# Output projection of a hybrid decoder block in seven quadrant products, on one Trainium2 core

## The chip, the cores and the metric
The kernel runs on one core of a Trainium2 chip. The metric is the device time of one execution in microseconds, the median of several runs. The engines are TensorE (PE, its weight load PEld), VectorE (DVE), ScalarE (ACT), GpSimd (POOL) and SyncE (SP), which here only issues transfers. Transfers issued by SP go over one queue of the core's 16 DMA engines, those issued by GpSimd over another.

## The reference
One decoder block on 512 tokens of width 1024, in float32. What matters here is the end of the mixer and what comes behind it:
```python
merged = jax.nn.sigmoid(gate_r) * y_ret + jax.nn.sigmoid(gate_m) * y_m
return merged @ w_out                      # (512, 1024) @ (1024, 1024)
...
x = x + mixer(...)                         # then RMSNorm, and per token:
group_prob = softmax(xf @ w_group + b_group)          # top 1 of 4 groups
e_logits = xf @ w_expert_router + b_expert_router     # top 2 of 8 experts in it
# per expert: (silu(xb @ w_gate[e]) * (xb @ w_up[e])) @ w_down[e], weighted and added to x
```
Before the mixer's end stand a wide input projection, a retention and an mLSTM, each with a branch projection of 1024 x 1024. There are 32 experts with 1024 x 512, 1024 x 512 and 512 x 1024 weights: 201 MB of float32, read once.

## The kernel before
A float32 product is made of three matmuls on rounded operands: each operand is split into a head (rounded to float32r, on ScalarE) and a tail (the rest, on VectorE), and head x head, head x tail and tail x head are added up in PSUM.

Weights for the projections stream in chunks of 512 x 512 (1 MB) over SP's queue into three places (`raw_mix`). Each half of a chunk (256 x 512, two slices of 128 rows) is a ring entry: `mix_head(q)` on ScalarE writes the head to `wh`, `mix_tail(q)` on VectorE the tail to `wl`, both in a ring of `RING` = 4 entries, running `LEAD` = 3 entries ahead of TensorE. An entry's place in the ring is free when TensorE has used the entry four before it (`entry_used`). A block is 512 output columns: 4 entries (j), 4 tiles of 128 rows (i), with the PSUM banks `pj[0..3]`. Blocks 16 to 21 are the branch projections `B_WR`, `B_WM` and the output projection `B_WO`, two blocks each. The projection blocks before them (`FAST`) already run in another form: a 1024 x 1024 product is cut into quadrants and made of seven products of quadrants (`U_11` to `U_T4`, Winograd's form of Strassen's method), 14 entries in place of 16 per pair of blocks, and four sums of weight quadrants each, some on VectorE (`weight_sum`), one by a transfer issued on GpSimd that adds to its place while it lands (`accum_op`).

When a block of `B_WM` ends, VectorE gates its four tiles into `sgm`, adds them into `mrg` (channels x tokens, 8 slices of 128 channels), ScalarE makes the heads `mrgTh` and VectorE the tails `mrgTl`, tile by tile (`merged_tail`). The two blocks of `B_WO` multiply these with `w_out`; VectorE adds each bank to the stream `x2`, tile by tile, at the end of each block. Then TensorE turns the four tiles of the stream (`turn_stream`, 8 turns each), VectorE and ScalarE copy the turned tiles to `h2T`, `logits(u)` makes the router's logits for half of the tokens, ScalarE copies them, `logit_rows(u)` turns them back. A routing chain on VectorE and TensorE makes the tables of the experts' tokens.

Experts are worked off in 16 pairs. A pair needs 12 chunks of 1 MB: 4 of `w_gate`, 4 of `w_up`, 4 of `w_down`. 22 places of 8 KB per partition (`raw_moe`) and one more (`guest`, for chunk 4) take them; chunk m goes to place m, one lower above 4, and the places lie on memory of tensors that are dead by then: `mrg`, the ring, `mrgTh` and so on. SP issues chunks in a written order (`moe_chunk`), each after a wait for what lay there. SP's instructions are strictly in order, so a wait holds back all chunks behind it. From chunk 22 on a chunk waits until TensorE has used the one 22 before it. The stream is also stored to DRAM (`x_dram`), from where GpSimd gathers each pair's tokens.

## Time and profile before

| | us |
|---|---|
| median of 3 runs (1022.3 to 1024.0) | 1023.38 |
| the profiled execution | 1022.9 |
| its span, first to last instruction | 1021.0 |
| TensorE busy | 996.3 (98%) |
| VectorE, ScalarE, GpSimd busy | 500.1, 323.9, 120.8 |
| DMA | 269.28 MB, mean 264 GB/s |

Times in the rows are from the start of the span. The profiled execution's own time is 1.9 us over its span, so a difference in the span is one in the time. The time falls into the projections with the mixers (to 535 us), the router (to 561) and the experts. The mean granted clock of TensorE is 0.996 of full speed. Matmuls are pipelined, so a busy TensorE may still be waiting for its operands in part; the DMA share is the mean over the 16 engines.

### The profile page before, as it was taken

The numbers are of one execution on the slowest core, as the hardware profiler recorded it, in microseconds if no ns is written. First come the engines' busy times: TensorE is split into PE (matmuls) and PEld (weight loads), VectorE is DVE, ScalarE is ACT, GpSimd is POOL, SyncE is SP. The second block draws the span as 40 slices with busy tenths as digits, with TensorE's granted clock in tenths as the row PEclk, the third lists the DMA queues.
The fourth block names the chain that finished last, engine by engine and source line by source line (L and its number), as shares of the span: only waits on it lengthen the run. The fifth ranks groups of instructions, "written<-read, shape, count | busy, mean of one in ns | idle before, by whom it ended". The sixth has DMA issues, their size and how long they took to land.

```text
span 1021.0 us, 13126 instructions
## 1 busy us (share of the span) xinstructions
PE 996.3 (98%) x4917; PEld 644.4 (63%) x4917; DVE 500.1 (49%) x810; ACT 323.9 (32%) x531; POOL 120.8 (12%) x152
## 2 busy tenths in 40 slices
PE   8999999999999999999998999999999999999896
PEld 7888788889889988888885333333333333333332
DVE  6268646597778677735525123333223233332235
ACT  6344535586556557622213100000000000000012
POOL 0683077000000000000000000000000000000000
PEclk9999999999999999999999999999999999999999
DMA  9223231344334525162988899999999999999993
GB/s 331 83 83 126 92 114 21 83 125 145 66 91 113 185 42 205 43 213 90 422 307 357 348 420 420 420 420 420 420 420 420 421 420 420 420 421 421 421 414 146
DMA packets 63125, 269.28 MB, mean 264 GB/s; under 512 B 9488, under 2 KB 9680, under 8 KB 38360
## 3 DMA queue, kind: packets, MB, share of 16 engines
q1 hardware_dynamic: 57464, 257.32, 63.6%
q0 software_dynamic: 5344, 11.02, 4.9%
q8 instruction: 41, 0.67, 0.3%
q14 instruction: 20, 0.16, 0.0%
q10 hardware_dynamic: 256, 0.10, 0.0%
HBM read 268.41 MB, written 4.20 MB: 267 GB/s over the span
## 4 chain that ended last, share of the span: by engine, by line
PE 72%; SPq 17%; DVE 5%; DMA 3%; ACT 2%; issue 1%; DVEq 0%; ACTq 0%
PE pj L674 23%; PE pj L854 18%; PE pj L956 12%; SPq L575 11%; PE pj L982 6%; SPq L572 6%; PE cb L631 3%; DMA raw_moe<-in_w_up_dram 3%; PE cb L992 2%; PE cb L993 1%; DVE mkT L1758 1%; DVE wl L1494 1%; PE cb L723 1%; PE cb L695 1%; ACT wh L1136 1%
## 5 line engine op out<-in xcount | busy, mean ns | idle before, releaser
L956 PE MATMUL pj<-raw_moe,xT 128*64 128x512 f32 x1016 | 227.6, 595 | 4.2 <-DMA raw_moe<-in_w_up_dram 2.4
L1494 DVE TENSOR_TENSOR wl<-raw_mix,wh 128x1024 fp32r<-128x1024 f32 x116 | 146.2, 1262 | 130.9 <-ACT wh L1136 130.6
L1970 DVE TENSOR_TENSOR x<-x,cb 128x512 f32<-128x512 f32 x120 | 77.0, 683 | 190.2 <-PE cb L993 190.2
L956 PEld LDWEIGHTS pj<-raw_moe,xT 128*64 128x64 f32 x1016 | 72.1, 137 | 140.8 <-issue 140.8
L1136 ACT ACTIVATE wh<-raw_mix 128x1024 fp32r<-128x1024 f32 x116 | 122.4, 1057 | 111.4 <-PE pj L674 68.5
L982 PE MATMUL pj<-raw_moe,hf 128*64 128x512 f32 x512 | 116.7, 598 | 1.6 <-ACT hf L1440 1.6
L982 PEld LDWEIGHTS pj<-raw_moe,hf 128*64 128x64 f32 x512 | 34.6, 136 | 67.2 <-issue 67.0
L1445 ACT ACTIVATE yh<-pj,now 128x512 fp32r<-128x512 f32 x32 | 20.4, 683 | 157.6 <-PE cb L993 143.6
L1440 ACT ACTIVATE hf<-cb 128x512 f32<-128x512 f32 x16 | 9.6, 598 | 146.3 <-PE cb L631 146.3
L992 PE MATMUL cb<-yh,hot 128*128 128x512 f32 x124 | 55.2, 445 | 0.0
L674 PE MATMUL pj<-wh,hTh 128*128 128x512 f32 x128 | 50.8, 397 | 1.7 <-DVE hTl L1525 0.7
L1975 DVE TENSOR_TENSOR xT<-cb,nwc 128x512 f32<-128x512 f32 x32 | 21.9, 687 | 58.0 <-PE cb L631 58.0
L674 PE MATMUL pj<-wl,hTh 128*128 128x512 f32 x128 | 49.9, 390 | 0.0
L674 PE MATMUL pj<-wh,hTl 128*128 128x512 f32 x128 | 49.9, 390 | 0.0
L993 PE MATMUL cb<-yl,hot 128*128 128x512 f32 x124 | 49.2, 397 | 0.0
L1436 ACT ACTIVATE sg<-pj,now 128x512 f32<-128x512 f32 x16 | 11.0, 688 | 100.7 <-PE pj L956 90.0
L992 PEld LDWEIGHTS cb<-yh,hot 128*128 128x128 f32 x124 | 23.6, 190 | 29.0 <-issue 26.2
L854 PE MATMUL pj<-wh,hTh 128*128 128x512 f32 x96 | 39.0, 406 | 0.7 <-DVE mva L1811 0.7
L854 PE MATMUL pj<-wl,hTh 128*128 128x512 f32 x96 | 37.6, 391 | 0.0
L854 PE MATMUL pj<-wh,hTl 128*128 128x512 f32 x96 | 37.4, 390 | 0.0
L854 PE MATMUL pj<-hTh,wh 128*128 128x256 f32 x128 | 36.5, 285 | 0.0
L1986 DVE SCALAR_TENSOR_TENSOR sg<-pj,now,sg 128x512 f32<-128x512 f32 x16 | 12.0, 751 | 49.5 <-PE pj L956 49.5
(397 smaller groups left out, 1858.5 us busy)
## 6 DMA issues: line engine op xcount, KB each, us to landing
raw_moe<-in_w_gate_dram SPq DMA_DIRECT2D x64, 1024.0 KB, 26.7
raw_moe<-in_w_down_dram SPq DMA_DIRECT2D x64, 1024.0 KB, 26.7
raw_moe<-in_w_up_dram SPq DMA_DIRECT2D x63, 1024.0 KB, 26.0
raw_mix<-in_w_in_dram SPq DMA_DIRECT2D x31, 1024.0 KB, 5.3
raw_mix<-in_w_in_dram POOLq DMA_DIRECT2D x10, 512.0 KB, 5.8
raw_mix<-in_w_ret_branch_dram SPq DMA_DIRECT2D x4, 1024.0 KB, 5.8
raw_mix<-in_w_mlstm_branch_dram SPq DMA_DIRECT2D x4, 1024.0 KB, 5.5
raw_mix<-in_w_out_dram SPq DMA_DIRECT2D x4, 1024.0 KB, 5.1
```

The lines of the kernel that those rows point to most:

```text
L572: sp.dma_start(weights_of(m)[:, :, :].rearrange("p (f c) n -> p f (c n)", f=2), w_down[0][e].rearrange("(a p f) n -> p a f n", a=2, f=2)[: ...
L575: sp.dma_start(weights_of(m)[:, :, :], (w_gate, w_up)[kind][0][e].rearrange("(a p k) n -> p a k n", a=2, k=4)[:, half, :, :]).then_inc(lan ...
L631: return nc.tensor.transpose(o, i, kc[0:k, K_IDENT:K_IDENT + k])
L674: m = nc.tensor.matmul(pj[:, i, :], lhsT, rhs, start=k == 0 and n == 0, stop=k == KD - 1 and n == 2)
L854: m = nc.tensor.matmul(o, lhsT, rhs, start=u in (U_11, U_21, U_T1) and k == 0 and c == 0 and n == 0, stop=k == 3 and n == 2, skip_group_ch ...
L956: mm = nc.tensor.matmul(pj[a * CAP:(a + 1) * CAP, up, :], xT[:, 4 * half + k, a * CAP:(a + 1) * CAP], weights_of(m + a)[:, k, :], start=ha ...
L982: mm = nc.tensor.matmul(pj[a * CAP:(a + 1) * CAP, 2 + c, :], hf[:, 2 * half + f, a * CAP:(a + 1) * CAP], weights_of(m + a)[:, 2 * f + c, : ...
L992: nc.tensor.matmul(bank, hot[:, t * P:(t + 1) * P], yh[:, c * 512:(c + 1) * 512], start=begin, stop=False)
L993: return nc.tensor.matmul(bank, hot[:, t * P:(t + 1) * P], yl[:, c * 512:(c + 1) * 512], start=False, stop=True)
L1136: nc.scalar.activation(wh[:, q % RING, :, :], entry_source(q), ACT.Copy).then_inc(wh_ok, 1)
L1494: V.tensor_tensor(wl[:, q % RING, :, :], entry_source(q), wh[:, q % RING, :, :].bitcast(F32), ALU.subtract).then_inc(wl_ok, 1)
L1970: V.tensor_tensor(part, part, cb[:, 2 + g % 2, :], ALU.add).then_inc(c_add, 1)
```

## The change
The output projection is no longer two blocks but seven products of quadrants, 14 ring entries. TensorE takes them in the order `U_11`, `U_21`, `U_T1`, `U_22`, `U_T2`, `U_T3`, `U_T4`, each for two tiles of 128 tokens (s). Activations now are seven parts, split whole (128 x 1024 elements) in place of tile by tile: `out_part_head(n)` on ScalarE, `out_part_tail(n)` on VectorE. Four of them are sums or differences of merged parts: VectorE makes two (`out_part_sum`), and GpSimd two more from them (`combined`, 4 operations each).

Of the weights seven places are loaded: four products' bases go to places of the experts' chunks (`out_slot`: 12, 13, 0, 1) during the branch projections, three to `raw_mix`. Seven sums (`out_sums`) are made by 14 transfers of half a chunk, issued on GpSimd, each after the one before has landed. No sum of weights is on VectorE.

The chunks' order on SP is rewritten to the places' new lives: chunks 13, 14, 0 and 1 come after the entries that use their places, 7 and 8 after the seventh tail, and so on. The results of four quadrants are collected in PSUM and in the stream by VectorE; two banks pass through a copy (`t1c`) on ScalarE. Two tiles of the stream are turned inside `U_T3`, the first logits are made inside `U_T4`.
```diff
 FAST_HALVES = FAST_ENTRIES
-ENTRIES = 4 * (BLOCKS - 2 * len(FAST)) + FAST_ENTRIES
+OUT0 = 4 * (BLOCKS - 2 * len(FAST)) + FAST_ENTRIES
+ENTRIES = OUT0 + 2 * PRODUCTS
...
-                   enumerate([64, 72, 0, 8, 16, 24, 80, 88, 144.0625, 152.0625, 104, 120, TOP, TOP + 8, 32, 40, 48, 56, 96, 112, 194.5625, 186.0625])]
+                   enumerate([64, 72, 0, 8, 16, 24, 80, 88, 144.0625, 152.0625, 96, 112, TOP, TOP + 8, 32, 40, 48, 56, 104, 120, 194.5625, 186.0625])]

...
+        out_slot = {U_11: 12, U_T1: 13, U_T2: 0, U_T4: 1}
+        out_sums = (U_T1, U_T2, U_T2, U_T4, U_T4, U_T4, U_T3)
+
+        def out_place(u):
+
+            return raw_moe[out_slot[u]] if u in out_slot else raw_mix[slot_of(2 * B_WO + (U_T3, U_22, U_21).index(u))]
...
+            def out_load(u, c):
+
+                sp.dma_start(out_place(u)[:, :, :], w_out[0][0:512, 512 * c:512 * (c + 1)].rearrange("(k p) n -> p k n", p=P))\
+                    .then_inc(moe_in[out_slot[u]], 16)
...
+            for n in range(2 * B_WR, 2 * B_WO + 3):
+                if n == 2 * B_WR + 3:
+                    sp.wait_ge(full[1], full_fast(len(FAST) - 1, U_T2, 1))
+                    out_load(U_11, 0)
+                    out_load(U_T1, 1)
+                if n == 2 * B_WR + 4:
+                    sp.wait_ge(tr_ps, KD)
+                    out_load(U_T2, 1)
+                    out_load(U_T4, 1)
                 if n == 2 * B_WM + 2:
...
-            moe_chunk(13, 0, False)
-            moe_chunk(14, 0, False)
             sp.wait_ge(it_ok, 1)
             moe_chunk(21, 0, False)
-            sp.wait_ge(tr_ps, KD)
-            moe_chunk(0, 0, False)
-            moe_chunk(1, 0, False)
-            sp.wait_ge(full[3], full_of(3, B_WO - 1))
-            for m in (2, 3, 5, 6):
-                moe_chunk(m, 0, False)
-            sp.wait_ge(mgl_ok, KD)
+            sp.wait_ge(wl_ok, out_entry(U_11, 1) + 1)
+            moe_chunk(13, 0, False)
+            sp.wait_ge(wl_ok, out_entry(U_T1, 1) + 1)
+            moe_chunk(14, 0, False)
+            sp.wait_ge(mgl_ok, 7)
             moe_chunk(7, 0, False)
             moe_chunk(8, 0, False)
-            sp.wait_ge(wl_ok, ENTRIES)
+            sp.wait_ge(wl_ok, out_entry(U_T2, 1) + 1)
+            moe_chunk(0, 0, False)
+            sp.wait_ge(*out_full(U_T2, 1))
+            for m in (2, 3, 5):
+                moe_chunk(m, 0, False)
+            sp.wait_ge(tr_l, 2 * KD + 2)
+            moe_chunk(6, 0, False)
+            sp.wait_ge(wl_ok, out_entry(U_T3, 1) + 1)
             moe_chunk(9, 0, False)
             moe_chunk(10, 0, False)
-            sp.wait_ge(*entry_used(ENTRIES - 3))
-            for m in (11, 12, 15, 17):
-                moe_chunk(m, 0, False)
             for t in range(TT):
-                sp.wait_ge(free[t], free_of(t, BLOCKS - 1))
+                sp.wait_ge(*tile_ready(t))
                 sp.dma_start(x_dram[t * P:(t + 1) * P, :], x2[:, t, :]).then_inc(st_in, 16)
-            for m in (16, 18, 19, 20):
+                if t == 1:
+                    sp.wait_ge(wl_ok, out_entry(U_T4, 1) + 1)
+                    moe_chunk(1, 0, False)
+                    sp.wait_ge(*out_full(U_T3, 1))
+                    moe_chunk(15, 0, False)
+                    moe_chunk(17, 0, False)
+            for m in (11, 12, 16, 18, 19, 20):
                 moe_chunk(m, 0, False)
             sp.dma_start(irow[:, :], consts[:, K_ROW:K_ALL]).then_inc(br_in, 16)
             sp.wait_ge(lg_ps, 2)
...
                 m.then_inc(lg_ps, 1)

-            pe.wait_ge(tr_l, 2 * KD)
-            for t in range(TT):
-                turn_stream(t)
-            pe.wait_ge(wrt_ok, 1)
-            logits(0)
+            out_parts = ((mrgTh[:, low, lower], mrgTl[:, low, lower]), (mrgTh[:, high, lower], mrgTl[:, high, lower]), (e5h, e5l), (e3h, e3l), (s2h, s2l),
+                         (mrgTh[:, low, upper], mrgTl[:, low, upper]), (mrgTh[:, high, upper], mrgTl[:, high, upper]))
+
+            def out_half(u, s):
+
+                if u == U_11:
+                    pe.wait_ge(*out_free(s, 0))
+                if u == U_21:
+                    pe.wait_ge(*out_free(2 + s, 0))
+                if u == U_22:
+                    pe.wait_ge(tr_h, 2 * KD + s + 1)
+                if u in (U_T2, U_T3, U_T4):
+                    pe.wait_ge(*out_free(s, (U_T2, U_T3, U_T4).index(u) + 1))
+                if s == 0:
+                    pe.wait_ge(mgl_ok, (1, 3, 4, 5, 6, 2, 7)[u])
+                ah, al = out_parts[u]
+                o = cb[:, s, :] if u in (U_T1, U_22) else pj[:, 2 + s, :] if u == U_21 else pj[:, s, :]
+                rows = slice(s * P, (s + 1) * P)
+                for v in range(2):
+                    q = out_entry(u, v)
+                    if s == 0:
+                        pe.wait_ge(wl_ok, q + 1)
+                    for kk in range(2):
+                        k = 2 * v + kk
+                        ops = ((ah[:, k, rows], wh[:, q % RING, kk, :]), (al[:, k, rows], wh[:, q % RING, kk, :]),
+                               (ah[:, k, rows], wl[:, q % RING, kk, :]))
+                        for n, (lhsT, rhs) in enumerate(ops):
+                            m = nc.tensor.matmul(o, lhsT, rhs, start=u in (U_11, U_21, U_T1) and k == 0 and n == 0,
+                                                 stop=k == 3 and n == 2, skip_group_check=True)
+                    if v == 1:
+                        m.then_inc(out_full(u, s)[0], 1)
+                    elif s == 1:
+                        m.then_inc(pair_used, 1)
+
...
+                    out_half(u, s)
+                    if u == U_T3:
+                        turn_stream(s)
+                    if u == U_T4 and s == 0:
+                        pe.wait_ge(wrt_ok, 1)
+                        logits(0)
+            turn_stream(2)
+            logit_rows(0)
+            turn_stream(3)
             logits(1)
-            logit_rows(0)
             logit_rows(1)

             def stay_awake(n):
...
+            def out_part_head(n):
+
+                if n in (0, 2, 6):
+                    act.wait_ge(mg_ok, 4 if n == 0 else KD)
+                if n == 0:
+                    act.wait_ge(*entry_used(entry(B_WM, 0) - 1))
+                if n in (1, 3):
+                    act.wait_ge(sum_ok, 6 * len(FAST) + (1 if n == 1 else 2))
+                if n in (4, 5):
+                    act.wait_ge(rope_ok, 2 * TT + 4 + (2 if n == 4 else 1))
+                lower, upper = slice(0, 256), slice(256, 512)
+                dst, src = ((mrgTh[:, 0:4, lower], mrg[:, 0:4, lower]), (mrgTh[:, 0:4, upper], mrgTf[:, 0:4, upper]), (mrgTh[:, 4:8, lower], mrg[:, 4:8, lower]),
+                            (e5h, e5f), (e3h, e3f), (s2h, s2f), (mrgTh[:, 4:8, upper], mrg[:, 4:8, upper]))[n]
+                nc.scalar.activation(dst[:, :, :], src[:, :, :], ACT.Copy).then_inc(mgh_ok, 1)
+
...
+            for x in range(2 * PRODUCTS):
+                if x == 0:
+                    out_part_head(2)
+                if x in (2 * U_T1 + 1, 2 * U_T1 + 2):
+                    out_copy(x - 2 * U_T1 - 1)
+                if OUT0 + x + LEAD < ENTRIES:
+                    mix_head(OUT0 + x + LEAD)
+                if x == 0:
+                    out_part_head(3)
+                if x in (3, 4, 5):
+                    out_part_head(x + 1)
+                if x == 2 * U_T3 + 1:
+                    square(0)
+                    stream_copy(0)
+                if x == 2 * U_T4:
...
+            def out_part_sum(n):
+
+                dve.wait_ge(mg_ok, 4 if n == 0 else KD)
+                lower, upper = slice(0, 256), slice(256, 512)
+                dst, one, two = ((mrgTf[:, 0:4, upper], mrg[:, 0:4, lower], mrg[:, 0:4, upper]), (e5f, mrg[:, 0:4, upper], mrg[:, 4:8, upper]))[n]
+                V.tensor_tensor(dst[:, :, :], one, two, ALU.subtract).then_inc(sum_ok, 1)
+
+            def out_part_tail(n):
+
+                dve.wait_ge(mgh_ok, n + 1)
+                if n in (4, 5):
+                    dve.wait_ge(rope_ok, 2 * TT + 6)
+                lower, upper = slice(0, 256), slice(256, 512)
+                dst, src, head = ((mrgTl[:, 0:4, lower], mrg[:, 0:4, lower], mrgTh[:, 0:4, lower]), (mrgTl[:, 0:4, upper], mrgTf[:, 0:4, upper], mrgTh[:, 0:4, upper]),
+                                  (mrgTl[:, 4:8, lower], mrg[:, 4:8, lower], mrgTh[:, 4:8, lower]), (e5l, e5f, e5h), (e3l, e3f, e3h), (s2l, s2f, s2h),
+                                  (mrgTl[:, 4:8, upper], mrg[:, 4:8, upper], mrgTh[:, 4:8, upper]))[n]
+                V.tensor_tensor(dst[:, :, :], src[:, :, :], head[:, :, :].bitcast(F32), ALU.subtract).then_inc(mgl_ok, 1)

             def out_tail(n):
...
+            for x in range(2 * PRODUCTS):
+                if x in (9, 10):
+                    upper_right_last(x - 9)
+                if x in (11, 12):
+                    lower_right_last(x - 11)
+                    stream_turned(x - 11)
+                if x == 13:
+                    lower_left(0)
+                if OUT0 + x + LEAD < ENTRIES:
+                    mix_tail(OUT0 + x + LEAD)
+                if x == 0:
+                    out_part_tail(2)
+                    out_part_tail(3)
+                if x in (1, 2):
+                    first_sum(x - 1)
+                if x in (3, 4):
+                    out_part_tail(x + 1)
+                if x == 5:
+                    second_sum(0)
+                    second_sum(1)
+                    out_part_tail(6)
+                if x == 6:
+                    router_weights()
+                if x == 7:
+                    lower_right_first(0)
+                    lower_right_first(1)
+                if x == 8:
+                    upper_right_first(0)
+                    upper_right_first(1)
...
+
+            for n, u in enumerate(out_sums):
+                if n == out_sums.index(u):
+                    pool.wait_ge(*(landed(2 * B_WO) if u == U_T3 else (moe_in[out_slot[u]], 16)))
+                k, c = (1, 1) if u == U_T3 else ((0, 0), (1, 1), (1, 0))[n - out_sums.index(u)]
+                for v in range(2):
+                    pool.wait_ge(gd_out, 16 + 32 * len(FAST) + 16 * (2 * n + v))
+                    pool.dma_start(out_place(u)[:, 2 * v:2 * v + 2, :],
+                                   w_out[0][512 * k + 256 * v:512 * k + 256 * (v + 1), 512 * c:512 * (c + 1)].rearrange("(k p) n -> p k n", p=P),
+                                   accum_op=ALU.add).then_inc(gd_out, 16)
+            pool.wait_ge(sum_ok, 6 * len(FAST) + 2)
+            combined(s2f, e5f, ((mrg[:, low, lower], ALU.subtract),))
+            pool.wait_ge(rope_ok, 2 * TT + 5)
+            combined(e3f, s2f, ((mrg[:, high, lower], ALU.add),))
```

## Rows read from the trace of the kernel before

**Rows 1.** The page's 40 slices of 25.5 us: DMA share in tenths, GB/s.
```profile
DMA  9223231344334525162988899999999999999993
GB/s 331 83 83 126 92 114 21 83 125 145 66 91 113 185 42 205 43 213 90 422 307 357 348 420 420 420 420 420 420 420 420 421 420 420 420 421 421 421 414 146
```

**Rows 2.** Windows: stretch; PE, PEld, DVE, ACT, POOL busy; clock, DMA share, GB/s.
```profile
475.00:480.00 5.00, 5.00 (x24) 4.14 (x23) 3.35 (x7) 1.51 (x2) 0.00 (x0) 1.00 0.28 66
480.00:515.00 35.00, 35.00 (x156) 29.01 (x155) 18.75 (x26) 9.71 (x11) 0.00 (x0) 1.00 0.94 380
515.00:570.00 55.00, 52.41 (x295) 34.56 (x296) 19.07 (x64) 12.11 (x22) 2.61 (x3) 0.97 0.80 308
560.00:565.00 5.00, 4.61 (x26) 2.29 (x26) 1.29 (x2) 0.00 (x0) 1.03 (x1) 1.00 0.21 61
567.00:997.00 430.00, 421.94 (x1904) 165.90 (x1900) 133.40 (x213) 41.06 (x64) 19.77 (x44) 1.00 1.01 420
...
535.00:540.00 5.00, 5.00 (x44) 4.44 (x44) 3.32 (x7) 4.22 (x9) 0.00 (x0) 1.00 0.96 367
```

**Rows 3.** Chain of waits at its turns: start us, us, what.
```profile
750.27 3.54 SPq L572
...
927.96 27.92 DMA raw_moe<-in_w_up_dram
...
956.13 3.66 PE pj L956 x16
...
1004.30 1.91 PE pj L1082 x4
```

**Rows 4.** TensorE's waits, 560 to 1021 us: total, times, longest.
```profile
PE pj L956 <- DMA raw_moe<-in_w_up_dram: 2.4, 2, 1.3
```

**Rows 5.** Chain of waits from the projections to the routing.
```profile
439.47 95.23 PE pj L674 x420
...
534.71 1.93 PE cb L631 x16
...
538.57 3.60 PE cb L900 x32
542.17 1.16 PE cb L909 x8
```

**Rows 6.** Timeline of VectorE and ScalarE around 491 us.
```profile
491.83 1.29 DVE L1696 TENSOR_TENSOR mrg<-mrg,sgm 128x512 f32<-128x512 f32 x2
...
497.36 2.36 DVE L1494 TENSOR_TENSOR wl<-raw_mix,wh 128x1024 fp32r<-128x1024 f32 x2 [0.25 <-ACT wh L1136]
...
502.16 1.06 ACT L1136 ACTIVATE wh<-raw_mix 128x1024 fp32r<-128x1024 f32 x1 [3.89 <-PE pj L674]
```

**Rows 7.** Groups of instructions, 490.8 to 534.5 us.
```profile
L1720 DVE TENSOR_TENSOR wrt<-wrt,nwc 128x288 f32<-128x288 f32 x1 | 0.5, 450 | 0.0
```

**Rows 8.** Timeline of the load queue: issues of chunks.
```profile
477.35 5.77 SPq L489 DMA_DIRECT2D raw_mix<-in_w_out_dram  x2
483.16 0.98 SPq L575 DMA_DIRECT2D raw_moe<-in_w_gate_dram  x2
...
492.06 5.40 SPq L575 DMA_DIRECT2D raw_moe<-in_w_up_dram  x3
```

**Rows 9.** Timeline, ScalarE and VectorE: a late branch chunk, the block's end.
```profile
454.31 1.06 ACT L1136 ACTIVATE wh<-raw_mix 128x1024 fp32r<-128x1024 f32 x1 [5.49 <-DMA raw_mix<-in_w_mlstm_branch_dram]
...
469.46 0.69 DVE L1683 TENSOR_TENSOR sgm<-pj,sgm 128x512 f32<-128x512 f32 x1 [0.67 <-PE pj L674]
```

**Rows 10.** The gathers (L2171) from issue to landing.
```profile
DMA to landing us min/median/max: 3.4/8.3/9.7
```

**Rows 11.** Groups of GpSimd: adding transfers, their waits, operand sums.
```profile
L2152 POOL DMA_DIRECT2D raw_mix<-in_w_in_dram x10 | 12.2, 1219 | 186.2 <-DVE raw_mix L1654 161.4 <-DMA raw_mix<-in_w_in_dram 24.8
L2130 POOL TENSOR_TENSOR thirdf<-thirdf,hTl 128x256 f32<-128x256 f32 x8 | 9.7, 1239 | 0.2
```

**Rows 12.** Issues of the branch chunks (L489), first and last.
```profile
L489 SPq DMA_DIRECT2D raw_mix<-in_w_ret_branch_dram x4: 368/368/368, 383.7 to 396.4; - x4
```

More of the change, by code:

```diff
@@ L403, in entry_ready @@
                 return sum_ok, 6 * p + 2 * (U_T1, U_T2, U_T4).index(u) + v + 1
+            if q >= OUT0:
+                u, v = divmod(q - OUT0, 2)
+                if u == U_11:
+                    return moe_in[out_slot[u]], 16
+                if u in (U_21, U_22):
+                    return landed(2 * B_WO + (U_T3, U_22, U_21).index(u))
+                last = max(n for n, w in enumerate(out_sums) if w == u)
+                return gd_out, 16 + 32 * len(FAST) + 16 * (2 * last + v + 1)
             n = q // 2 if q < 4 * F0 else (q - FAST_ENTRIES + 8 * len(FAST)) // 2
@@ L462, in wait_chunk @@
             loads = (R_CHUNKS - 2 - s) // MOE_RAW + 1
[L463 removed]
+            eng.wait_ge(moe_in[s], r * (16 * loads) + 16 * (place(m) // MOE_RAW + 1 + (s in out_slot.values())))
         @block.sync
```

158 lines of the change are left out of this document (106 added, 52 removed).

## The prediction

> **What bounds the kernel now.** I read the page's slices first. TensorE is busy in nearly every slice, but from the slice at 560 us on the DMA rate stands at 420 GB/s and does not move again until the last slice but one [rows 1]. So I asked for stretches. From 567 to 997 us the core moves 420 GB/s with the engines' share at 1.01: that is the ceiling, and the 192 expert chunks of 1 MB fill most of it. In front of that it is not at the ceiling: 380 GB/s in 480 to 515 us, 308 in 515 to 570, and only 61 in 560 to 565, where every place for a chunk is full and TensorE has just started on the experts [rows 2].
>
> The chain of waits then says which of the two decides. Up to about 750 us it runs through TensorE, from there through the queue that issues the chunks, and its last DMA step is a chunk that lands at 955.88; behind it TensorE works without a gap to 1004.3 and the tail follows [rows 3]. TensorE waits little for the chunks, 2.4 us in all for those of `w_up`, the longest such wait [rows 4]. So both limits lie close together, but the transfer limit is the later one. The reader is to see this: once the transfers are at their ceiling, the end is where the remaining bytes put it. A microsecond saved on TensorE in the output projection gives nothing unless the chunks are also fetched earlier; a chunk fetched later costs 1.0486 MB / 420 GB/s = 2.5 us, unless a hole such as that at 560 us takes it up.
>
> **The matmuls.** The old projection has 2 blocks x 4 entries x 4 tiles x 2 x 3 = 192 matmuls of 512 columns; 420 such take 95.23 us, 0.227 us each [rows 5], so it takes 43.5 us, from 491.2 to 534.7, where that piece of the chain ends. The new one has 7 products x 2 row tiles x 4 x 3 = 168: 38.1 us, a saving of 5.4 us. One product is 24 matmuls, 5.44 us.
>
> **Its first wait.** The second product (`U_21`) needs the third tail, that of the high half of `mrg`. Its last inputs are four additions into `mrg`, from 491.8 at 0.6 each, two in 1.29 us with their overlap [rows 6], so 494.3. ScalarE then does head 2 (1.06) and the split of ring entry 3 (1.06), 496.4. VectorE in that time does the new sum (1.22), then the tail of ring entry 3 (1.22, to 497.6) and tail 2 (1.2), 498.8. The durations are those of the 128x1024 rows [rows 6]. TensorE starts the projection at 491.2 at the latest, finishes `U_11` at 496.6 and waits 2.2 us. Queued behind it is the whole projection. From then on I step product by product with the same durations. The ring gives each later entry in time, so `U_T1` starts at 504.2, `U_22` at 509.7, `U_T2` at 515.1. `U_T3` needs the upper right sum: VectorE is through with tail 6 at 513.3 (below), then come three ring tails (3.7), the router weights (0.45 and two shorter ones, 0.8 together [rows 7]) and five sums at 0.6, 521.0 in place of 520.6. Two turns (half of 1.93 us each) lie inside, then `U_T4` with the first logits (1.8 us, half of 3.60) between its halves, to 535.8; turns 2 and 3, ScalarE's last copy (0.6), logits 1, copy and rows: about 542.3. Before, the logit rows end at 542.17 + 1.16 = 543.3 [rows 5]. Of the 5.4 us, 2.2 go into the wait, 0.4 before `U_T3`, and some 1.8 into copies that used to lie beside other matmuls: 1.0 us is left.
>
> **What moves on the load queue.** This is the costly part. SP's queue is in order, and each chunk's place is now freed later. In the kernel before, ten chunks are issued from 483.2 to 497.5 [rows 8]. In the new order chunk 21 can go at 477 and chunk 13 at 482.8, chunk 14 waits for ring entry 5 (503 by the same steps), and chunks 7 and 8 wait for the seventh tail, with chunks 0, 2, 3, 5 and 6 queued behind them although some of their places are free earlier. The seventh tail: ring entry 8 is free when `U_T1` has used entry 4, 504.2 + 4.1 = 508.3. Head and tail of it (1.06 + 1.22) give 510.8, two second sums (0.6 each) 512, tail 6 513.3. So by 515 us (with about 1.5 us from issue to steady flow) the new kernel has fetched 3 chunks, 3.15 MB. From there its queue never empties: 3 chunks at 513 to 515, 6 more by 521, 3 more and the stream's stores by 536.5, 7 after that; to 570 us that is 55 us x 420 GB/s = 23.1 MB. Together 26.2 MB.
>
> The old kernel moved 35 x 380 + 55 x 308 = 30.2 MB from 480 to 570 us [rows 2]. Of this 1.77 MB are the last two chunks of `w_out` (2.10 less the 0.33 that 475 to 480 carried), so 28.5. The new kernel is 2.3 MB behind when both are at the ceiling: **5.4 us**. The hole around 560 has taken up the rest of the gap. From 570 on both are at the ceiling, so this lateness is passed on whole to the chunk at the end of the chain and to what follows it. The bounds: without the wait at `U_21` everything moves 2.2 us earlier, 3.2 us are left; if steps between heads and tails cost 0.1 us more each (some ten of them) and the stores keep the rate at the 367 GB/s of 535 to 540 [rows 2] for 5 us, it is 7.0.
>
> **Costed at nothing.** The four extra plain loads of `w_out` parts (4.2 MB) and the 14 adding transfers (7.3 MB) run from about 396 to 495 us, where few chunks are due; the branch weights that they meet, for which ScalarE waits 5.5 us, are split at 456.6, while TensorE turns to them when the block before ends, at 469.4 [rows 9]. If the cover were gone, each would cost its lateness directly. The first gather meets a full queue (8.3 us, the median, rather than 3.4, the shortest [rows 10]), so TensorE starts the experts up to 4 us later; it has that slack, as the transfers finish last. The expert phase itself is unchanged.
>
> **The adding transfers.** A half chunk takes 1.22 us to issue on GpSimd and then 4.9 (24.8 us of waits / 5) to land, 6.1 in series [rows 11]. The first part is issued after the third branch chunk, before 396.4 [rows 12], and is there by 405, so 14 of them end at 405 + 85.4 = 490.4; the two new operands (8 operations of up to 1.24 us) need GpSimd from 495.5 and are wanted by about 507, which holds to 505.5. What the trace of before doesn't show is such a transfer beside the slice from 434 to 459 us, in which loads already hold half of the engines [rows 1], and the 5 us behind it. Nearest row: a gather of the same size takes 4.9 us more in a full queue; by that the series ends 12 us later, 502.5. Between these ends I take 497, which costs nothing yet, and keep the other as a rival. The Trainium skill, DMA: Bandwidth & Descriptors, section "Issuing engines are not separate DMA queues", says that transfers of all issuing engines run on the same 16 DMA engines and interleave, which speaks for that rival; no row here shows it for adding ones. The same page's fit (2.0 us plus bytes at 436 GB/s, section on the anatomy of one DMA) gives an estimate of 3.2 us for 512 KB where the row has 4.9; by it the series would end 24 us sooner and this rival would fall, but the measured row goes before it.
>
> **The sum.** On the profiled execution: 1022.9 (span 1021.0) + 5.4 = 1028.3. The median of the runs is 0.5 above that execution, so **1028.8 us**.
>
> **Rivals.**
> - *The transfers aren't the bound; the experts follow the routing* (0.11). For it: TensorE is busy nearly throughout and waits little for chunks. Against it: 430 us at the ceiling. Then the end moves with the routing, 1.0 us earlier, 1022.4, and 1020.2 if the wait at `U_21` isn't there either. It decides once the lateness of the loads is under zero, that is if tail 6 comes before 508 us. This is the side on which the change is not slower.
> - *No wait at `U_21`*, the head and tail finish in time (0.09): 3.2 us late, 1026.6.
> - *GpSimd is late* (0.18): its series ends at 502.5, the operand for `U_22` at 512.5, its tail at 515 rather than before 509.7. `U_22` then waits 5.3 us, tail 6 comes at 518.5 and all later chunks with it: 1034.
> - The load queue as computed (0.62): 1026.5 to 1031.
>
> **Range and chances.** A difference of 0.2%, 2 us, is about what a measurement of this kernel can tell from none. Low end 1023.0: a part of the first rival stays outside. High end 1034.5: GpSimd late is inside. Slower by over 0.2% (over 1025.4): the second and third rival and nearly all of the main case, 0.82. Within 0.2%: some of the first and the low edge of the others, 0.09. Faster (under 1021.3): 0.09. The main case alone: 1026.5 to 1031.
>
> **What would show it.** In the changed kernel's trace: 168 matmuls at 0.227 us between about 491 and 536; a gap of 2 to 3 us before the second product; the chunks' queue idle between 485 and 513 but for one; no hole at 560; saturation from 515 to about 1003; the last DMA step of the chain 4 to 7 us later than 955.9, and the work behind it equal. Wrong would be: chunks 7 and 8 issued before 509, TensorE's start on the experts deciding the end, or a rate above 420 GB/s after 515. If GpSimd's operations on the merged parts begin after 500, the third rival has come.

## The result and the profile after

The changed kernel takes 1040.45 us (median of 4 runs, 1038.82 to 1044.11) against 1022.89 for the kernel before beside it: a ratio of 1.0175, 95% interval 1.0146 to 1.0204. The forecast of 1028.8 had the side right, but the time lies 5.95 us above its range (1023.0 to 1034.5). The profiled execution took 1044.11, its span is 1042.2, that is 21.2 more than before.

The page's slices of the changed kernel, in the form of [rows 1], and windows with the columns of [rows 2]:
```profile
DMA  9224322434243348797479999999999999999993
GB/s 325 81 81 147 108 70 32 130 82 163 41 158 86 123 119 250 201 271 194 101 308 411 407 421 420 420 421 419 420 421 420 419 421 421 419 420 421 421 411 133
```
```profile
480.00:515.00 35.00, 27.77 (x122) 22.37 (x120) 18.18 (x20) 8.03 (x8) 7.91 (x9) 0.99 0.65 156
515.00:570.00 55.00, 44.94 (x253) 32.11 (x254) 34.01 (x81) 22.42 (x33) 3.64 (x5) 0.91 0.81 319
560.00:565.00 5.00, 2.80 (x35) 1.27 (x34) 4.13 (x17) 0.20 (x1) 0.00 (x0) 1.00 1.03 428
567.00:997.00 430.00, 415.81 (x1889) 164.43 (x1888) 127.13 (x206) 38.65 (x61) 21.74 (x45) 0.99 1.01 420
...
510.00:520.00 10.00, 0.00 (x0) 0.00 (x0) 1.39 (x2) 2.48 (x3) 6.75 (x9) 0.72 0.33 52
520.00:525.00 5.00, 4.00 (x10) 3.18 (x11) 5.00 (x6) 4.27 (x6) 0.00 (x0) 0.54 0.00 0
```
From 567 us on nothing has changed: 420 GB/s, the ceiling. The loss lies ahead of it. From 480 to 515 us the core moves 156 GB/s instead of 380, and between 510 and 520 TensorE does not run at all. The twentieth slice, from 495 to 521 us, stands at 101 GB/s; in [rows 1] the twentieth, from 485 to 510 us, stands at 422.

GpSimd's timeline says why (start, us, operation, and in brackets the idle time ahead of it with its releaser):
```profile
401.17 1.21 POOL L2387 DMA_DIRECT2D raw_moe<-in_w_out_dram  x1 [30.57 <-DMA raw_moe<-in_w_out_dram]
407.92 1.22 POOL L2387 DMA_DIRECT2D raw_moe<-in_w_out_dram  x1 [5.53 <-DMA raw_moe<-in_w_out_dram]
...
451.49 1.21 POOL L2387 DMA_DIRECT2D raw_moe<-in_w_out_dram  x1 [9.28 <-DMA raw_moe<-in_w_out_dram]
462.61 1.22 POOL L2387 DMA_DIRECT2D raw_moe<-in_w_out_dram  x1 [9.91 <-DMA raw_moe<-in_w_out_dram]
...
510.65 1.21 POOL L2387 DMA_DIRECT2D raw_mix<-in_w_out_dram  x1 [6.36 <-DMA raw_mix<-in_w_out_dram]
511.41 3.24 POOL L2355 TENSOR_TENSOR s2f<-e5f,mrg 128x256 f32<-128x256 f32 x4
514.72 2.76 POOL L2355 TENSOR_TENSOR e3f<-s2f,mrg 128x256 f32<-128x256 f32 x4
```
Fourteen issues lie between 401.17 and 510.65, 8.4 us apart on average. Two of the steps as windows, a short one and a long one:
```profile
434.16:440.99 6.83, 6.83 (x36) 5.73 (x35) 3.12 (x5) 2.33 (x3) 1.21 (x1) 1.00 0.60 91
440.99:451.49 10.50, 10.50 (x48) 8.71 (x47) 5.26 (x7) 2.12 (x2) 1.22 (x1) 1.00 1.03 257
```
A step takes 6.8 to 7.6 us where at most 1.0 MB of other loads moves in it (seven steps), and 9.0 to 11.1 where 1.5 to 2.6 MB do (six steps; megabytes summed from the packets of the load queue). The two operands of the merged parts, behind them in the queue, are ready at 517.5. ScalarE and VectorE stand still for them, and with them everything that is queued behind:
```profile
517.52 1.06 ACT L1362 ACTIVATE e3h<-e3f 128x1024 fp32r<-128x1024 f32 x1 [14.00 <-POOL e3f L2355]
...
520.37 0.57 ACT L1545 ACTIVATE t1c<-cb 128x512 f32<-128x512 f32 x1
```
```profile
518.61 1.23 DVE L1746 TENSOR_TENSOR e3l<-e3f,e3h 128x1024 fp32r<-128x1024 f32 x1 [13.83 <-ACT e3h L1362]
...
524.35 1.22 DVE L1746 TENSOR_TENSOR mrgTl<-mrg,mrgTh 128x1024 fp32r<-128x1024 f32 x1
```
TensorE's waits, 480 to 600 us:
```profile
PE cb L1017 <- ACT t1c L1545: 11.8, 1, 11.8
PE cb L707 <- DMA xg<-x_scratch,tok_tab: 6.0, 1, 6.0
PE pj L1017 <- issue: 1.4, 1, 1.4
```
The first names `t1c`, a copy of 0.57 us. It isn't the cause: it stood behind the head of `e3f` in ScalarE's queue, and that waited for GpSimd. The third ends at 498.0, where `U_21` starts. The seventh tail ends at 525.6 instead of 513.3, and the load queue shows what it held back (SP's issues):
```profile
482.75 19.52 SPq L645 DMA_DIRECT2D raw_moe<-in_w_gate_dram  x2
525.60 0.33 SPq L645 DMA_DIRECT2D raw_moe<-in_w_up_dram  x1
...
544.91 5.16 SPq L674 DMA_DIRECT2D x_scratch<-x  x2
...
567.85 17.02 SPq L642 DMA_DIRECT2D raw_moe<-in_w_down_dram  x2
```
Chunks 21, 13 and 14 go out by 502.3 us, then none for 23.3 us. The chain of waits at the experts' start and at its end:
```profile
549.74 16.88 DMA x_scratch<-x
567.60 9.19 DMA xg<-x_scratch,tok_tab
578.90 15.84 PE pj L1073 x64
...
967.88 29.11 DMA raw_moe<-in_w_gate_dram
997.23 3.65 PE pj L1073 x16
```
The last store of the stream needs 16.9 us to land behind the backlog of chunks, the first gather then 9.2, and the experts start at 578.9 instead of 561.3, 17.6 us later.

### The profile page after: what moved, and what is told of

Its sections match the earlier page's. It is cut to its first block, busy times and chain, and to the rows that moved or that the text cites. A ratio compares the mean times of both kernels' runs of the same rounds, so it can differ in the third digit from the quotient of the medians.

```text
span 1042.2 us, 13144 instructions
## 1 busy us (share of the span) xinstructions
PE 995.6 (96%) x4893; PEld 641.5 (62%) x4893; DVE 516.0 (50%) x823; ACT 332.8 (32%) x538; POOL 143.1 (14%) x174
## 4 chain that ended last, share of the span: by engine, by line
PE 72%; DMA 15%; SPq 5%; DVE 4%; ACT 2%; issue 2%; POOL 1%; DVEq 0%; POOLq 0%; ACTq 0%
PE pj L1073 19%; PE pj L928 18%; PE pj L750 11%; PE pj L1099 9%; DMA raw_moe<-in_w_out_dram 9%; PE cb L707 3%; DMA raw_moe<-in_w_gate_dram 3%; PE cb L1109 3%; SPq L645 2%; PE cb L1110 2%; SPq L642 2%; DMA x_scratch<-x 2%; PE pj L1017 2%; DMA xg<-x_scratch,tok_tab 1%; DVE sg L2211 1%
## 5 line engine op out<-in xcount | busy, mean ns | idle before, releaser
L1639 DVE TENSOR_TENSOR wl<-raw_mix,wh 128x1024 fp32r<-128x1024 f32 x114 | 143.8, 1262 | 121.4 <-ACT wh L1253 121.0
L1590 ACT ACTIVATE yh<-pj,now 128x512 fp32r<-128x512 f32 x32 | 20.4, 683 | 158.2 <-PE cb L1110 143.8
L750 PE MATMUL pj<-wh,hTl 128*128 128x512 f32 x128 | 49.9, 390 | 0.0
L2406 POOL COPY tok_now<-tok_tab 128x1 int32 x14 | 2.6, 187 | 263.9 <-PE cb L707 263.9
L2377 POOL DMA_DIRECT2D raw_mix<-in_w_in_dram x10 | 12.2, 1219 | 186.3 <-DVE raw_mix L1813 161.3
L707 PEld LDWEIGHTS cb<-kc,xg 128*128 128x128 f32 x128 | 18.4, 211 | 31.2 <-issue 31.2
```

The costliest lines, as they stand in the source:

```text
L707: return nc.tensor.transpose(o, i, kc[0:k, K_IDENT:K_IDENT + k])
L750: m = nc.tensor.matmul(pj[:, i, :], lhsT, rhs, start=k == 0 and n == 0, stop=k == KD - 1 and n == 2)
L1639: V.tensor_tensor(wl[:, q % RING, :, :], entry_source(q), wh[:, q % RING, :, :].bitcast(F32), ALU.subtract).then_inc(wl_ok, 1)
```

## A measure for all runs

Two things are late in the changed kernel, the fetched bytes and the experts' start. To tell them apart I took from each profiled run (1) what all DMA queues together still move from 600 us on, as time at 420 GB/s against before (169.8 MB), (2) the start of the experts against 561.27, (3) the span against 1021.0. All are us, but for the megabytes, which are summed from the packets.

| kernel | median | bytes late | experts late | span longer |
|---|---|---|---|---|
| changed kernel | 1040.5 | 19.8 | 17.6 | 21.2 |
| GpSimd's operands first | 1038.2 | 15.4 | 14.2 | 15.4 |
| two chains | 1045.3 | 20.4 | 18.3 | 22.2 |
| stores from ScalarE | 1042.1 | 15.1 | 12.5 | 16.0 |
| before, late loads | 1034.6 | 11.7 | 10.2 | 11.8 |
| the same, stores from ScalarE | 1031.5 | 7.5 | 3.2 | 8.6 |
| two chains, new order | 1040.8 | 17.9 | 17.0 | 18.0 |
| the same, no turns inside | 1041.8 | 21.5 | 19.5 | 21.9 |
| operands on VectorE | 1033.8 | 6.1 | 3.7 | 7.9 |
| the same, new order | 1033.6 | 10.2 | 9.0 | 10.1 |
| and the third sum on VectorE | 1028.6 | 5.8 | 3.7 | 5.8 |
| the same, no turns inside | 1031.2 | 8.3 | 6.3 | 8.5 |
| and the first gather free | 1027.8 | 4.7 | 0.8 | 4.9 |

In every run the span is longer by the bytes' lateness, to within 2 us. Since every run moves its bytes at the same rate behind 600 us (402 to 404 GB/s on average to its end), this says that nothing behind 600 us costs or gives back time; it doesn't say what made the bytes late. The experts' start alone misses by 4 to 5.5 us in three runs: in the late loads with stores from ScalarE (3.2 against 8.6), with the operands on VectorE (3.7 against 7.9) and in the last line (0.8 against 4.9). That speaks against the forecast's rival in which the experts merely follow the routing. So the forecast's rule, the end is where the remaining bytes put it, holds. What it lacked is that the experts' start is one of the things that make bytes late: where all places are full before it, nothing is fetched until it comes.

## The experiments

**First group.** The changed kernel, with GpSimd's operands moved ahead of the last three transfers, the sums of `U_T3` and the last half of `U_T4`'s:
```diff
-            for n, u in enumerate(out_sums):
...
+            for n, (u, k, c, v) in enumerate(out_sums):
+                if n == 11:
+                    pool.wait_ge(sum_ok, 6 * len(FAST) + 2)
+                    combined(s2f, e5f, ((mrg[:, low, lower], ALU.subtract),))
+                    pool.wait_ge(rope_ok, 2 * TT + 5)
+                    combined(e3f, s2f, ((mrg[:, high, lower], ALU.add),))
```


> The changed kernel, but GpSimd makes its two merged operands after 11 of the 14 adding transfers, and the three left are those wanted last (both halves of U_T3's, the last of U_T4's second half). If the 12.3 us wait at U_22 comes from GpSimd's series alone, it falls to under 3 us, the seventh tail comes at 513 to 515 instead of 525.6, and by the load theory (the end moves with the bytes fetched by 570 us) the time is 1027 to 1031. Rival, the series wasn't what U_22 waited for: time stays at 1038 to 1042. Second rival, the three late sums are wanted before they land and the wait only moves to U_T3: about 1034.

1038.2 us, ratio 1.0163 (1.0131 to 1.0196). The wait at `U_22` is gone and the seventh tail starts at 513.39. But the late transfers now meet the chunks, and ScalarE waits for them twice:
```profile
524.07 1.06 ACT L1254 ACTIVATE wh<-raw_mix 128x1024 fp32r<-128x1024 f32 x1 [7.61 <-DMA raw_mix<-in_w_out_dram]
525.03 1.04 ACT L1254 ACTIVATE wh<-raw_moe 128x1024 fp32r<-128x1024 f32 x1
536.74 1.06 ACT L1254 ACTIVATE wh<-raw_moe 128x1024 fp32r<-128x1024 f32 x1 [10.67 <-DMA raw_moe<-in_w_out_dram]
```
The second rival came, and dearer than its 1034: TensorE's longest wait is now 6.1 us, for a sum of VectorE that stands behind the first of these heads. The new order only moved the wait.

The changed kernel without the 14 adding transfers (the weight sums are left out):
```diff
-                for v in range(2):
-                    pool.wait_ge(gd_out, 16 + 32 * len(FAST) + 16 * (2 * n + v))
-                    pool.dma_start(out_place(u)[:, 2 * v:2 * v + 2, :],
...
```


> The changed kernel without its 14 adding transfers: the weight sums of the output projection are left out, so the entries are split as soon as the bases have landed. GpSimd is free at 490. Load theory: as with the operands made early, the wait at U_22 is gone, 1026 to 1030, and the difference to that run is what the adding transfers cost by their 7.3 MB alone. If these bytes delay the branch weights, this is 2 us or more under that run; if they lie in idle places, as the prediction had it, within 1 us.

This was a badly chosen run: other logits route other tokens, and the experts' weights are loaded twice over (128 loads of `w_gate` instead of 64), which makes 1520.8 us. Only the part up to the routing can be read. There the wait at `U_22` is gone, and the seventh tail starts at 513.27. ScalarE's wait for the late branch chunk is 5.48 us, as in [rows 9]; with the adding transfers it is 9.21; the projection starts at 491.85 without and 491.03 with them. So in this pair of profiles their bytes in the branch phase cost nothing, as costed.

The changed kernel with the stream's four stores issued from ScalarE's queue:
```diff
-                sp.dma_start(x_dram[t * P:(t + 1) * P, :], x2[:, t, :]).then_inc(st_in, 16)
...
+                act.dma_start(x_dram[t * P:(t + 1) * P, :], x2[:, t, :]).then_inc(st_in, 16)
```


> The changed kernel, but the four stores of the stream are issued from ScalarE's queue, not behind the chunks in SP's. It separates what sets the end. Load theory: the first gather lands up to 10 us earlier than 576.8 and TensorE starts the experts that much earlier than 578.9, but the end stays within 2 us of 1040.4, as the same bytes are fetched at the same ceiling. Rival, the experts' start sets the end: 1031 to 1034.

1042.1 us, ratio 1.0187 (1.0170 to 1.0204): the end is not earlier, as the load theory has it. In the profiled execution the experts start 5.1 us earlier (573.8), but 3.8 of these come from its wait at `U_22`, which happened to be 8.0 us. So in the changed kernel the stores' place behind the chunks costs little, and the "up to 10 us" that I had expected for the start were wrong.

The kernel before with its chunks held back:
```diff
             sp.wait_ge(tr_ps, KD)
+            sp.wait_ge(wl_ok, ENTRIES)
             moe_chunk(0, 0, False)
```


> The kernel before, with all chunks but 13, 14 and 21 held back until the last ring entry is split (about 515 us), as the output projection's new order does; nothing else is changed. It measures the step for the load queue alone. Load theory: three chunks by 515, then the ceiling; 5.4 us more than before, 1028 (3.2 to 7). Rival, the end follows the experts' start and not the bytes: no more than the start is later.

1034.6 us, ratio 1.0109 (1.0092 to 1.0126), 11.5 us more. The step that I had priced at 5.4 costs twice that. Its windows:
```profile
560.00:570.00 10.00, 0.51 (x3) 0.54 (x4) 0.00 (x0) 0.00 (x0) 1.12 (x1) 0.71 1.01 422
570.00:580.00 10.00, 9.98 (x41) 4.18 (x41) 1.58 (x3) 0.00 (x0) 1.22 (x2) 0.78 0.64 240
```
By 570 us it is 3.1 MB behind, 7.5 us, where I had 2.3 MB: from 515 to 570 us it moves 22.2 MB (403 GB/s), where I had put 23.1 at the full rate. Then comes a hole of 4 us: all places are full and the experts haven't begun. TensorE waits 10.6 us for the first gather, which stands behind the stores, and they behind the backlog.

**Second group: what makes the hole, and can the series be split?** First the kernel before with late loads, and its stores issued from ScalarE by the edit above:

> The kernel before with its chunks held back to 515 us as in the run on late loads (1034.6), and the stream's stores issued from ScalarE instead of behind the chunks in SP's queue. In that run the chunks' bytes were 7.5 us late by 570 us, and 4 us more were lost in a hole from 570 to 580 us, in which all places were full and TensorE waited 10.6 us for its first gather. If the stores behind the backlog make that hole, it closes: 1029.5 to 1031.5. Rival, the stores aren't the cause (they land as late, as the engines are full anyway): 1033.5 to 1035.

1031.5 us, ratio 1.0084 (1.0067 to 1.0101), 3.2 us less than with the stores behind the chunks: the hole is gone (417 GB/s from 570 to 580) and TensorE waits 1.5 us for the gather. The experts start 3.2 us late, the end is 8.6 late: here the bytes alone decide.

The changed kernel with two chains of adding transfers:
```diff
-                    pool.wait_ge(gd_out, 16 + 32 * len(FAST) + 16 * (2 * n + v))
+                    pool.wait_ge(*((gd_two, 16 * n) if v else (gd_out, 16 + 32 * len(FAST) + 16 * n)))
...
```


> The changed kernel, but the adding transfers run as two chains, one for each half of the places, with a semaphore each, so two are under way at a time; nothing else is changed. GpSimd theory: the last one is issued before 480 instead of at 510.65, the operands of the merged parts are made from 495.5, the wait of 12 us at U_22 and any wait for late sums are gone; the seventh tail comes at 513 to 515. Late chunks and the hole behind 570 us (as in the kernel before with late loads, 11.5 us) remain: 1031 to 1035. If only the wait at U_22 had cost, 1028. Rival, two adding transfers at once take twice as long each: no change, 1038 to 1042.

1045.3 us, ratio 1.0216 (1.0199 to 1.0233), not better. GpSimd keeps its old pace, though each transfer now waits for the last but one only. The second waits for nothing by the code, whatever releaser its line names, and still goes 6.6 us behind the first:
```profile
401.85 1.21 POOL L2388 DMA_DIRECT2D raw_moe<-in_w_out_dram  x1 [31.49 <-DMA raw_moe<-in_w_out_dram]
408.44 1.22 POOL L2388 DMA_DIRECT2D raw_moe<-in_w_out_dram  x1 [5.38 <-DMA raw_moe<-in_w_out_dram]
...
428.74 1.22 POOL L2388 DMA_DIRECT2D raw_moe<-in_w_out_dram  x1 [7.50 <-issue]
435.58 1.21 POOL L2388 DMA_DIRECT2D raw_moe<-in_w_out_dram  x1 [5.62 <-issue]
```
With the same two chains, the seventh part split earlier, the chunks issued in the order in which their places come free, and the stores from ScalarE:
```diff
...
+            sp.wait_ge(mgl_ok, 5)
+            go((7, 8), rope_ok, 2 * TT + 6)
+            go((10,), wl_ok, out_entry(U_22, 1) + 1)
+            go((2,), *out_full(U_T1, 1))
...
+            go((15, 17, 11, 12), *out_full(U_T3, 1))
+            go((16, 18, 19, 20), *out_full(U_T4, 1))
```


> The changed kernel with two chains of adding transfers, the seventh merged part split right behind the fourth, the chunks issued in the order in which their places become free (14, 7, 8, 10, 2, 0, 5, 6, 9, 3, 1, then 15, 17, 11, 12, then the rest), and the stores issued from ScalarE. Theory: eight chunks instead of three are issued by 515 us, no hole behind 565 us; the end is set by bytes and the experts' start together: 1020 to 1025. If the order of the chunks doesn't matter, as with two chains alone, 1031 to 1035.

1040.8 us, ratio 1.0162 (1.0137 to 1.0186): my 1020 to 1025 was wrong, because it leaned on the two chains. The wait at `U_22` is 12.3 us, and this order of the chunks doesn't give it back. The version without turns inside:
```diff
-                    if u == U_T3:
-                        turn_stream(s)
-                    if u == U_T4 and s == 0:
-                        pe.wait_ge(wrt_ok, 1)
-                        logits(0)
+            turn_stream(0)
+            turn_stream(1)
+            pe.wait_ge(wrt_ok, 1)
+            logits(0)
             turn_stream(2)
```


> As the version with two chains and the new order of the chunks, but no tile of the stream is turned inside the products and no logits are made there: all of it stands behind the last product. The part of the change that turns half of the stream inside is thereby undone. The routing begins 1.5 to 3 us later. If the end still follows the bytes, within 1 us of that version; if the experts' start sets it, 1.5 to 3 us more.

1041.8 us, ratio 1.0175 (1.0157 to 1.0193). The medians differ by 0.9 us, but the executions of each spread over 5 to 6: inconclusive. The question is put again below.

**Third group: the operands on another engine, and what is slow in the transfers.** The changed kernel, with the two operands made by VectorE instead of GpSimd:
```diff
+                dst, one, two, op = ((s2f, e5f, mrg[:, 0:4, lower], ALU.subtract), (e3f, s2f, mrg[:, 4:8, lower], ALU.add))[n]
+                V.tensor_tensor(dst[:, :, :], one[:, :, :], two, op).then_inc(rope_ok, 1)
...
-            combined(s2f, e5f, ((mrg[:, low, lower], ALU.subtract),))
-            pool.wait_ge(rope_ok, 2 * TT + 5)
-            combined(e3f, s2f, ((mrg[:, high, lower], ALU.add),))
```


> The changed kernel, but VectorE makes the two operands s2f and e3f (two operations of 1.22 us on 128x1024 behind the first sums) instead of GpSimd behind its adding transfers; the transfers, the chunks' order and the stores are those of the changed kernel. GpSimd theory: the wait of 12 us at U_22 falls to under 3 us, the seventh tail comes at 513 to 515 instead of 525.6. What stays is three chunks by 515 us and the hole behind 570 us, measured at 11.5 us in the kernel before with late loads: 1031 to 1035. If the last sum, which is in only at about 517, is wanted before, a wait of some us moves to U_T3: up to 1038.

1033.8 us (1029.9 to 1038.8), ratio 1.0116 (1.0074 to 1.0158). The wait at `U_22` is gone at a price of 2.4 us on VectorE, and the chunks behind the seventh tail are issued 12.8 us earlier than the 525.60 of the changed kernel:
```profile
512.82 0.33 SPq L645 DMA_DIRECT2D raw_moe<-in_w_up_dram  x1
```
This is the cleanest test of the third rival: 6.7 us of the loss by the medians; in the profiled pair the span falls by 13.3, so the size is uncertain by some 4 us or more: that profile is of an execution of 1030.8, and two others took 1036.7 and 1038.8. With the new order and the stores from ScalarE:

> As the version with the operands on VectorE, and besides the seventh merged part split before the fifth, the chunks issued as their places become free, and the stores issued from ScalarE. All three causes found so far are mended: the wait at U_22, the late issue of chunks (eight instead of three by 515 us), the stores behind the backlog. 1020 to 1026. If it stays above 1030, some cause is still unknown.

1033.6 us, ratio 1.0105 (1.0088 to 1.0122): above the 1030 that I had set as the mark for an unknown cause. It was the last adding transfer, issued at 507 us, when two chunks had just gone out (506 us); ScalarE waits for it, VectorE for ScalarE and TensorE 5.0 us for VectorE:
```profile
520.88 1.06 ACT L1244 ACTIVATE wh<-raw_mix 128x1024 fp32r<-128x1024 f32 x1 [6.47 <-DMA raw_mix<-in_w_out_dram]
```
```profile
PE pj L1008 <- DVE x L2080: 5.0, 1, 5.0
```
The chunks were earlier, and beside them the sum was late. With plain transfers in place of adding ones (the weight sums are not made):

> The version with two chains, with plain transfers in place of adding ones: the weight sums are not made, which changes the logits and so the routing, so only the time up to about 520 us is to be read. It asks why the two chains kept the pace of one (6.7 us from issue to issue at the least). If adding is what makes the transfers go one by one, GpSimd now issues each within 1.2 to 2 us of the one before it where both chains are free, and the 14 take 40 to 60 us instead of 117. If it is the issue on GpSimd or the size, the pace stays at 6.7 to 7.8 us.

GpSimd's timeline with them:
```profile
415.20 1.44 POOL L2388 DMA_DIRECT2D raw_moe<-in_w_out_dram  x2 [8.02 <-DMA raw_moe<-in_w_out_dram]
423.52 0.73 POOL L2388 DMA_DIRECT2D raw_moe<-in_w_out_dram  x1 [6.88 <-DMA raw_moe<-in_w_out_dram]
425.31 0.72 POOL L2388 DMA_DIRECT2D raw_moe<-in_w_out_dram  x1 [1.06 <-DMA raw_moe<-in_w_out_dram]
...
440.50 0.74 POOL L2388 DMA_DIRECT2D raw_moe<-in_w_out_dram  x1 [1.65 <-DMA raw_moe<-in_w_out_dram]
```
Two are issued back to back (x2), eight between 423.5 and 440.5, 2.4 us apart; the issue takes 0.73 us instead of 1.21. The first twelve are issued within 38 us, and the last two wait 24.3 us for the weights that they would be added to; the steps of 1.2 to 2 us that I had expected came only in part. So it is the adding that makes them slow and single, not GpSimd's issue nor the size. Why two adding ones did not overlap is not settled.

**Fourth group.** The sum of `U_T3` made by VectorE, since both its parts lie in the raw places anyway:
```diff
-        out_sums = (U_T1, U_T2, U_T2, U_T4, U_T4, U_T4, U_T3)
+        out_sums = (U_T1, U_T2, U_T2, U_T4, U_T4, U_T4)
...
+                            V.tensor_tensor(out_place(U_T3)[:, 2 * v:2 * v + 2, :], out_place(U_T3)[:, 2 * v:2 * v + 2, :], out_place(U_22)[:, 2 * v:2 * v + 2, :], ALU.add).then_inc(t3_ok, 1)
```


> As the version with VectorE's operands, the chunks by free places and the stores from ScalarE (1033.6), but U_T3's weight sum is made by VectorE from the two parts in the raw places (two operations, about 2.4 us in all) instead of by the last two adding transfers. There the last of them was issued at 507 us into a queue full of chunks and TensorE waited 5.0 us for what came of it. If that wait carries over to the experts' start and the end follows that start wherever all places are full before it, 5 us less: 1027 to 1029.5. If the end followed only the backlog of chunks, no change: 1032 to 1035.

1028.6 us, ratio 1.0052 (1.0038 to 1.0066): 5.0 us less, as expected. The edit also takes away two adding transfers, so their bytes are a rival. The packets speak against it: at 570 us the two versions have 184.1 and 183.9 MB left, 0.4 us apart, and at 600 us 174.1 and 172.2 MB, 4.4 us apart. The gain arises at the experts' start. Without turns inside:

> As the version with U_T3's sum on VectorE, but with all turning of the stream and the first logits behind the last product: the third part of the change undone, in a kernel whose end follows the experts' start. 1.5 to 3 us more than that version. Backlog theory: no change.

1031.2 us, ratio 1.0078 (1.0062 to 1.0093), 2.6 us more: the third part of the change is worth that, where the experts' start counts. And with the chunks held back for the gather:
```diff
-            go((16, 18, 19, 20), *out_full(U_T4, 1))
+            go((16,), *out_full(U_T4, 1))
...
             moe_chunk(GUEST, 0, False)
+            go((18, 19, 20), gat, 16)
             sp.wait_ge(cnt_ok, 2)
```


> As the version with U_T3's sum on VectorE, but chunks 18, 19, 20 and 22 are held back until the first gather has landed, so it meets a queue that runs empty, as in the kernel before (3.4 us to land rather than 8 to 9). If the time of the gather is part of the chain that starts the experts, 3 to 5 us less: 1023 to 1026. If the chunks held back cost as much as the start gains, no change.

1027.8 us, ratio 1.0047 (1.0033 to 1.0060). My 1023 to 1026 was not reached. The experts start at 562.04, 2.9 us earlier than in the run with `U_T3`'s sum on VectorE, but the end is only 0.9 earlier in the span. Its windows from 550 us:
```profile
550.00:560.00 10.00, 8.59 (x73) 4.37 (x74) 5.57 (x26) 1.49 (x2) 1.41 (x1) 0.83 0.64 250
560.00:570.00 10.00, 9.60 (x48) 4.44 (x48) 1.49 (x3) 0.69 (x1) 1.21 (x2) 1.00 0.99 389
```
The hole has moved ahead of the start and is nearly as big. No version that I ran beats the kernel before. The best one keeps seven products and ends some 5 us behind it: at 515 us it has 6.0 MB more left to move than the kernel before (205.4 MB against 199.4), and at 570 us still 2.0 MB (184.4 against 182.5), which is 4.7 us. The likely reason, which no run tested, is the places that hold weights and parts until they are used.

## Why the prediction failed, by its own steps

- **The kernel is bound by its transfers from 570 us on.** Right: the 13 versions of the table end where their bytes left at 600 us put them, within 2 us, also the three whose experts start almost in time.
- **Matmuls 192 to 168; the wait at `U_21`.** The projection starts at 491.03 (491.2 was said), and the wait is 1.4 us, not 2.2. In the run with `U_T3`'s sum on VectorE, where GpSimd's waits are away, the logit rows end at 543.28 + 0.64 = 543.9, against 542.3 forecast for a chain without its copies' small waits.
- **The adding transfers.** This is the step that failed first. I took 6.1 us each, by a wait from one sum of the input projection, and between 490.4 without any delay and 502.5 with the 4.9 us of a full queue in one dense stretch I took 497 for the end of the series. Alone they pace at 6.8, beside other loads at 9 to 11, and there was not one dense stretch: six of the thirteen steps lay beside loads (396 to 500 us: 213 GB/s, engines' share 0.81). The last issue came at 510.65. The third rival (0.18) was the case, with the right mechanism and queue: the wait at `U_22` was 11.8 us instead of 5.3, the tail 525.6 instead of 518.5. Its own sizes were off too: the series ran longer still, while the operands took 6.1 us instead of the 9.9 that the rival gave them, which hid some of it. Even its 1034 was 6.5 us short.
- **The load queue.** This term failed as well. 5.4 us (3.2 to 7.0) were given for the later issue of the chunks; made alone, in the kernel before, it costs 11.5 us. With GpSimd in time and the rest of the changed kernel as it is (operands on VectorE) 10.4 are left by the medians, so the main case of 1026.5 to 1031 would have been missed even then. In the kernel before with late loads the bytes were 7.5 late by 570, and 4 us stand in a hole that I had excluded with the words "it has that slack" about TensorE's later start.
- **Costed at nothing.** The loads and adding bytes in the branch phase cost nothing, as said. The first gather can cost: it waits for stores queued behind chunks, and I had counted how full the engines are and not what it waits for (the last store lands after 16.9 us). In the kernel before with late loads this is worth 3.2 us; in the changed kernel, moving the stores gave nothing back.
- **The marks.** "GpSimd's operations on the merged parts begin after 500" came true (511.4). No hole at 560: right. Saturation from 515 to the end: it came at about 540. The chain's last DMA step, said to end 4 to 7 us after 955.9 with equal work behind it, ends at 997.0, at another chunk and with 45 us behind it instead of 65: this mark could not be read as I had worded it. What moved by the lateness is the end of the expert loads themselves (the rate falls to 322 GB/s in 990 to 1000 us before, to 313 in 1010 to 1020 after).

In sum, of the 17.6 us by the medians some 7 (uncertain by 4 or more) go back with the operand's wait, 5 more with the late sum once the order is mended, and some 5 stay, put down to the late places without a test. The parts don't add up cleanly, since each mend moves the next one's collision.

## What to carry over

A series of adding transfers has to be timed beside the loads that will run with it, and nothing with a due time should stand behind it in its engine's queue. When loads are issued later, follow not only their bytes but also the small stores that share their queue, and what waits for those. Where all places fill up ahead of the next phase, the start of that phase sets the loads, so a load-bound kernel can still lose its time on an engine.

## What the runs showed of the hardware

- Adding transfers of 512 KB issued from GpSimd went one at a time here, 6.8 us apart alone and 9 to 11 beside other loads, also in two chains; plain ones of the same shape 2.4 us apart. From issue to landing the adding ones took 7.5 us and the plain ones 4.7 (medians of twelve). The fit in the Trainium skill, DMA: Bandwidth & Descriptors, section "Anatomy of one DMA", gives an estimate of 3.2 us for this size: both kinds took longer here, the adding ones more than twice as long.
- VectorE's operations on two SBUF operands of 128x1024 take 1.22 us when GpSimd does not compute and, in five of six cases, 1.75 to 1.80 while it does (the sixth, at 503.82, took 1.21); those with one operand in PSUM keep their 0.68. In the kernel with GpSimd's operands first:
```profile
496.47 1.80 DVE L1640 TENSOR_TENSOR wl<-raw_mix,wh 128x1024 fp32r<-128x1024 f32 x1 [0.81 <-ACT wh L1254]
...
503.23 0.68 DVE L2056 TENSOR_TENSOR x<-x,pj 128x512 f32<-128x512 f32 x1
```
  GpSimd's four operations for `e3f` take 5.72 us there, and 2.76 in the changed kernel, where VectorE is idle. The Trainium skill, SBUF — State Buffer, section "Who interferes with whom", says that a VectorE instruction with two inputs in SBUF contends with a GpSimd one that reads SBUF; this trace agrees.
- While TensorE stood idle before `U_22` its granted clock fell to 0.50 (516 to 520 us), and behind that wait it was still 0.54 from 520 to 525, close to the lower of its two levels (1.2 and 2.4 GHz); from 525 to 530 it was 1.00. The first matmuls behind the wait go 0.43 us apart, those from 524.85 on 0.23: over the eight steps from 521.00 to 524.58 that is 1.7 us on top of the wait.
